# A hybrid two-layer kernel on one core: the down and last projections by token ranges, with a range's norms placed beside the next range's products, and 1026 tokens instead of 1044 in the feed-forward

## The reference

```python
h = h + rms_norm(mix, mix_post_g)
xn = rms_norm(h, ffn_pre_g)
gu = xn @ w_up                                  # 1024 -> 2 * 2816
g = causal_dwconv(gu[..., :D_FF], ffn_conv_w, ffn_conv_b)       # 3 taps
f = (gelu(g, approximate=True) * gu[..., D_FF:]) @ w_down       # 2816 -> 1024
h = h + rms_norm(f, ffn_post_g)
x = h[:, N_META:]                               # first_block returns this
u = _rmsnorm(x, norm_w) @ w_in                  # the second layer
...                                             # gated linear attention, RWKV
x = x + merged @ w_out
return _rmsnorm(x, final_norm_w)
```

## Time and profile before

| | |
|---|---|
| median of 3 runs | 2700.62 us (2700.24 to 2700.97) |
| the profiled execution: its time, its span | 2705.07 us, 2703.3 us |
| mean granted clock of TensorE | 0.961 |
| busy: PE, PEld | 2486.1 us (92%), 1514.5 us (56%) |
| busy: DVE, POOL, ACT | 1265.1, 1102.5, 896.2 us |
| DMA | 164.79 MB, 61 GB/s on average |

### The profile page before, as it was taken

How to read it: one execution, slowest core, us unless ns; L and a number is a source line. 1 busy time by engine, 2 the same in 40 slices (tenths; PEclk the granted TensorE clock), 3 DMA queues, 4 the chain that set the end, 5 groups by cost and what they waited for, 6 DMA issues and landing times. The chain is left out here.

```text
span 2703.3 us, 44126 instructions
## 1 busy us (share of the span) xinstructions
PE 2486.1 (92%) x18196; PEld 1514.5 (56%) x18196; DVE 1265.1 (47%) x1204; ACT 896.2 (33%) x1528; POOL 1102.5 (41%) x784
## 2 busy tenths in 40 slices
PE   6999988999999989989999997999479999979986
PEld 3666655666666545656666664444124444568842
DVE  5665763434344455675444442000567746226513
ACT  3126754555555563441111111000144432114301
POOL 6453236565555642025444443333365433100141
PEclk8999999999999989999999998999789999979998
DMA  2122110000000013321111111110023541123231
GB/s 104 55 68 82 55 48 24 25 24 25 24 17 24 9 46 105 126 84 55 48 53 47 54 47 51 43 53 32 29 85 94 155 133 40 55 82 84 68 123 62
DMA packets 100039, 164.79 MB, mean 61 GB/s; under 512 B 25488, under 2 KB 71712, under 8 KB 98480
## 3 DMA queue, kind: packets, MB, share of 16 engines
q1 hardware_dynamic: 99888, 162.64, 18.9%
HBM read 136.86 MB, written 25.76 MB: 60 GB/s over the span
## 5 line engine op out<-in xcount | busy, mean ns | idle before, releaser
L1398 DVE TENSOR_TENSOR_SCAN att_kept<-att_keep 128x143 f32<-128x143 f32 (+7 forms) x128 | 171.0, 1342 | 315.0 <-ACT att_keep L1315 315.0
L214 PE MATMUL ps<-x_hi,whi_z 128*128 128x348 f16 x1008 | 313.0, 311 | 0.2 <-POOL wlo_z L188 0.2
L216 PE MATMUL ps<-x_hi,wlo_z 128*128 128x348 f16 x1008 | 312.6, 310 | 0.0
L215 PE MATMUL ps<-x_lo,whi_z 128*128 128x348 f16 x1008 | 312.1, 310 | 0.0
L1162 POOL TENSOR_TENSOR att_beta<-att_beta,att_kept 128x256 f32<-128x256 f32 (+7 forms) x128 | 195.6, 1528 | 221.7 <-DVE att_kept L1398 200.8
L2155 PE MATMUL ps<-second_x_hi,whi_second 128*128 128x512 f16 x480 | 183.9, 383 | 14.5 <-POOL second_x_lo L316 13.4
L1195 PE MATMUL ps<-x_hi,whi_z 128*128 128x348 f16 x576 | 181.1, 314 | 14.0 <-POOL wlo_z L1152 9.4
L2156 PE MATMUL ps<-second_x_lo,whi_second 128*128 128x512 f16 x480 | 183.7, 383 | 0.0
L2157 PE MATMUL ps<-second_x_hi,wlo_second 128*128 128x512 f16 x480 | 183.5, 382 | 0.0
L1196 PE MATMUL ps<-x_lo,whi_z 128*128 128x348 f16 x576 | 180.4, 313 | 0.0
L1197 PE MATMUL ps<-x_hi,wlo_z 128*128 128x348 f16 x576 | 180.4, 313 | 0.0
(11 more groups left out here) (483 smaller groups left out, 5829.0 us busy)
## 6 DMA issues: line engine op xcount, KB each, us to landing
wraw_z<-in_w_up SPq DMA_DIRECT2D x44, 512.0 KB, 3.5
wraw_second<-in_w_second SPq DMA_DIRECT2D x30, 512.0 KB, 3.6
wraw_z<-in_w_qkv SPq DMA_DIRECT2D x24, 512.0 KB, 3.6
wraw_down<-in_w_down SPq DMA_DIRECT2D x16, 704.0 KB, 4.0
second_work<-parked_units SPq DMA_DIRECT2D x8, 1280.0 KB, 7.0
seg<-dt_a_sums SPq DMA_DIRECT2D x18, 512.0 KB, 3.9
wraw_z<-in_w_out SPq DMA_DIRECT2D x18, 512.0 KB, 3.7
wraw_out<-in_w_out SPq DMA_DIRECT2D x18, 512.0 KB, 3.6
```

Of the source, the lines that this page charges most:

```text
L214: nc.tensor.matmul(out, hi, xhi, start=(k == 0), stop=False)
L215: nc.tensor.matmul(out, hi, xlo, start=False, stop=False)
L216: return nc.tensor.matmul(out, lo, xhi, start=False, stop=(k == L.parts * L.kb - 1))
L1398: nc.vector.tensor_tensor_scan(out[:, 1:t.keys], x, x, 1.0, ALU.mult, ALU.min).then_inc(s_scan, 1)
```

## The change

The part of the program before `w_out` is as it was. From there on:

1. **1026 tokens.** `w_out` and `w_up` are computed for the last two learned tokens and the 1024 real ones, three thirds of `FT` = 342 columns instead of 348; the products and their numbers are otherwise the same. The cuts of `f` are done in two halves of 512 tokens.
2. **Down by ranges.** `ffn_down_phase` replaces `linear_phase` and both norm phases. A unit is a weight column block and a token range: 8 units for range A (tokens 0 to 511), blocks 7 and 6 for B and C together (512 columns), six units of 256 columns for B, six for C. A unit's weights come in three parts (8, 8 and 6 blocks of 128) that each unit loads anew, except the one where the block stays the same; cuts are ACT's (high) and DVE's (low), in a ring of four; the first parts are loaded, the very first also cut, in `ffn_up_phase`. The steps of both norms of a range, by the `link_` functions, stand in the lists of ACT and DVE between the cuts of the units after it. Range C's are in `second_in_phase`, beside its first two weight blocks (`first_linears`). Both norms' sums over features are added up on ACT and DVE first, so a sum is one product with ones. `parked_h` is written range by range.
3. **The last projection by ranges.** In `rwkv_units_phase` the products of `w_out_2` run over tokens 0 to 511, 512 to 767, 768 to 1023, all eight blocks each; the weights' halves are all kept. The final norm of a range is beside the next range's products, and a range's result leaves block by block. The first two weight blocks are cut within the units (`c == NUNIT - 1`).
4. All semaphores of the second layer's last phase are cleared at the end of the program. The set-up of `x11` in `rwkv_units_phase` comes after two others.

```diff
+F0 = META - 2
+FT = (T - F0) // NT
+FW = NT * FT
...
             @block.sync
             def _(sp):
                 stream_weights(sp, L, 2 * FFB)
+                for s in range(SLOTS):
+                    sp.wait_ge(L.cut, 2 * FFB - SLOTS + s + 1)
+                    sp.dma_start(Ld.raw[:, s, :], Ld.w[0][:, s * SEQ:(s + 1) * SEQ]).then_inc(Ld.landed[s], 16)
             @block.gpsimd
             def _(pool):
                 cut_weights(nc, S, pool, L, 2 * FFB)
+                pool.wait_ge(L.products, done(L, 2 * FFB - SLOTS))
+                cut_first(nc, S, pool, Ld, 1)
...
+F_KEPT = 16
+LAST = SEQ // 4
+RANGES = {"A": slice(0, BANK), "BC": slice(BANK, SEQ), "B": slice(BANK, SEQ - LAST), "C": slice(SEQ - LAST, SEQ)}
+DOWN_UNITS = [(b, "A") for b in range(DB)] + [(DB - 1, "BC"), (DB - 2, "BC")]
+DOWN_UNITS += [(b, "B") for b in range(DB - 2)] + [(b, "C") for b in range(DB - 2)[::-1]]
+DOWN_PARTS = ((0, 8), (8, 16), (16, FFB))
+END_OF_A, END_OF_B = DB - 1, 2 * DB - 1
...
+            @block.sync
+            def _(sp):
+                for i in range(SLOTS):
+                    nc.sync.sem_inc(s_landed[i], 16)
+                for i in range(SLOTS, NL):
+                    if i >= RING:
+                        sp.wait_ge(s_cut, i - RING + 1)
+                    b, q = DOWN_LOADS[i]
+                    k0, k1 = DOWN_PARTS[q]
+                    sp.dma_start(w_raw(i), A["w_down"][b][:, k0 * P:k1 * P]).then_inc(s_landed[i % RING], 16)
+                    if i == fresh(END_OF_B - 1)[0]:
+                        sp.wait_ge(CA.added, DB)
+                        sp.dma_start(parked_h[:, :, RANGES["A"]], down[:, :, RANGES["A"]]).then_inc(s_parked_h, 16)
+                for s in range(SLOTS):
+                    sp.wait_ge(s_cut, NL - RING + s + 1)
+                    sp.dma_start(L.raw[:, s, :], L.w[s]).then_inc(L.landed[s], 16)
+                L.fetched = True
+                sp.wait_ge(CB.added, DB)
+                sp.dma_start(parked_h[:, :, RANGES["B"]], down[:, :, RANGES["B"]]).then_inc(s_parked_h, 16)
+                sp.wait_ge(s_parked_h, 2 * 16)
...
+                for u in range(len(DOWN_UNITS)):
+                    if u >= 6:
+                        pe.wait_ge(s_sq, u - 5)
+                    if u == END_OF_A + 3:
+                        link_sum(nc, S, pe, CA, 1)
+                    part(u, 0)
+                    if u == END_OF_A + 1:
+                        pe.wait_ge(s_acc, sums_by(END_OF_A))
+                        link_sum(nc, S, pe, CA, 0, ssq[:, RANGES["A"]])
+                    if u == END_OF_B + 1:
+                        pe.wait_ge(s_acc, sums_by(END_OF_B))
+                        link_sum(nc, S, pe, CB, 0, ssq[:, RANGES["B"]])
+                    if u == END_OF_B + 4:
+                        link_sum(nc, S, pe, CB, 1)
+                    part(u, 1)
+                    part(u, 2)
...
+                squares = {END_OF_A + 1: (CA, ((0, 1), (2, 3))), END_OF_A + 2: (CA, ((4, 5, 6), (7,), ())),
+                           END_OF_B + 1: (CB, ((), (0,), (1,))), END_OF_B + 2: (CB, ((2,), (3,), (4,))), END_OF_B + 3: (CB, ((5,), (6, 7), ()))}
+                roots = {(END_OF_A + 1, 0): (CA, 0), (END_OF_A + 3, 0): (CA, 1), (END_OF_B + 1, 1): (CB, 0), (END_OF_B + 4, 1): (CB, 1)}
+                highs = {END_OF_A + 3: (CA, ((0,), (1, 2), (3,))), END_OF_A + 4: (CA, ((4,), (5,), (6,))), END_OF_A + 5: (CA, ((7,), (), ())),
+                         END_OF_B + 4: (CB, ((), (), (0, 1))), END_OF_B + 5: (CB, ((2,), (3,), (4,))), END_OF_B + 6: (CB, ((5, 6), (7,)))}
...
+                def low(i):
+                    dve.wait_ge(s_whi, i + 1)
+                    nc.vector.scalar_tensor_tensor(w_lo(i), w_raw(i), WSCALE, w_hi(i), ALU.mult, ALU.subtract).then_inc(s_cut, 1)
...
-        with nc.sbuf_tensor("ffn_out", [P, DB, SEQ], F32) as down:
-            with Phase(nc) as layer:
-                L = linear_buffers(nc, layer, A["w_down"], 0, FFB // 2, "down", parts=2)
-                linear_phase(nc, S, L, lambda k: (S.fhi[:, k, :], S.flo[:, k, :]), DB, down, 2, BANK, META)
-            norm_phase(nc, S, "ffn_post", down, "ffn_post_g", DB, SEQ, ("add", S.h[:, :, META:T]), 2, BANK)
-
+        S.xhi, S.xlo = x
+        Ls = linear_buffers(nc, second, A["w_second"], 0, DB, "second", like=Lz)
+        down = second.enter_context(nc.sbuf_tensor("ffn_out", [P, DB, SEQ], F32))
+        ffn_down_phase(nc, S, A, Lz, Ld, Ls, down, rows, parked_h, s_parked_h)
...
+                    if i == 2 * SLOTS:
+                        sp.wait_ge(C.added, DB)
+                        sp.dma_start(parked_h[:, :, SEQ - LAST:SEQ], W.high[:, :, SEQ - LAST:SEQ]).then_inc(s_parked_h, 16)
...
+                def first_linears():
+                    nc.tensor.sem_inc(L.cut, SLOTS)
+                    pe.wait_ge(L.cut, SLOTS)
+                    link_sum(nc, S, pe, C, 0, ssq[:, SEQ - LAST:SEQ])
+                    for at, end in ((0, BANK), (BANK, SEQ - LAST), (SEQ - LAST, SEQ)):
+                        for i in range(SLOTS):
                             for j in range(DB):
-                                last = product(n, j)
-                    last.then_inc(s_lin, 1)
+                                if i == 0 and end == SEQ:
+                                    pe.wait_ge(C.low, j + 1)
+                                last = product(i, slice(at, end), j)
+                            if end == SEQ:
+                                last.then_inc(s_lin, 1)
+                            if i == 0 and end == SEQ - LAST:
+                                link_sum(nc, S, pe, C, 1)
...
+                first_linears()
                 for i in range(SECOND_B + 2):
-                    if i < SECOND_B:
+                    if i < SLOTS:
+                        pass
+                    elif i < SECOND_B:
...
+                link_root(nc, S, act, C, 0, DB)
+                for n in range(DB):
+                    link_square(nc, act, C, n)
+                link_root(nc, S, act, C, 1, DB)
+                for n in range(DB):
+                    link_high(nc, act, C, n)
...
+        spans = ((0, BANK), (BANK, BANK + BANK // 2), (BANK + BANK // 2, SEQ))
+        width = lambda i: spans[i][1] - spans[i][0]
+        done_units = (4, 6, 8)
...
+                    if c == NUNIT - 1:
+                        sp.wait_ge(s_glo, GLA_HEADS)
+                        fetch_first(sp, L)
+                        sp.dma_start(back, parked_h).then_inc(s_back, 16)
...
+                for i in range(len(spans)):
+                    for b in range(DB):
+                        sp.wait_ge(s_fin, i * DB + b + 1)
+                        sp.dma_start(out[:, b, toks(i)], back[:, b, toks(i)]).then_inc(s_result, 16)
+                sp.wait_ge(s_result, 16 * DB * len(spans))
...
+                    if c == NUNIT - 1:
+                        cut_first(nc, S, pool, L)
                     if c == NUNIT:
-                        cut_first(nc, S, pool, L)
+                        pool.wait_ge(s_yd, NUNIT)
+                        pool.wait_ge(s_rrc, NUNIT)
+                        cut(SLOTS)
...
+                def output(i, b):
+                    u = i * DB + b
+                    ps = bank(u % 4)[:, 0:width(i)]
+                    pe.wait_ge(L.cut, b + 1)
+                    if u >= 4:
+                        pe.wait_ge(s_res, u - 3)
+                    for j in range(DB):
+                        if b == 0 and j == RWKV_P:
+                            pe.wait_ge(s_lo, done_units[i])
+                        hi, lo = (w(b)[:, j * P:(j + 1) * P] for w in (w_hi, w_lo))
+                        xhi, xlo = (x[:, j, toks(i)] for x in merged)
+                        nc.tensor.matmul(ps, hi, xhi, start=(j == 0), stop=False)
+                        nc.tensor.matmul(ps, hi, xlo, start=False, stop=False)
+                        last = nc.tensor.matmul(ps, lo, xhi, start=False, stop=(j == DB - 1))
+                    last.then_inc(s_po, 1)
...
+                for i in range(len(spans)):
+                    for b in range(DB):
+                        output(i, b)
+                        if i == 0 and b == 0:
+                            variances(NUNIT - 1)
+                        if i and b == 1:
+                            square_sums(i - 1)
+                square_sums(len(spans) - 1)
...
+                for i in range(len(spans)):
+                    for b in range(DB):
+                        residual(i, b)
+                        if b >= 2:
+                            more(i, b - 1)
+                        if i and b >= 3:
+                            final(i - 1, b - 3)
...
-            rwkv_units_phase(nc, S, D, W, plast, L, merged, parked_h, back)
-        res = S.h_flat[:, 0:DB * SEQ].rearrange("p (a n) -> p a n", a=DB)
-        norm_phase(nc, S, "final", back, "final_norm_w_2", DB, SEQ, ("to", res, out, s_result), 2, BANK)
```

(21 more changed lines are left out.)

471 lines of the change are left out of this document (321 added, 150 removed).

## The result

2614.09 us (median of 4 runs, 2611.27 to 2615.34), against 2700.43 us for the kernel before in the same comparison (median of 4, 2695.04 to 2700.97): a ratio of 0.9671, 95% interval 0.9657 to 0.9685. That is 86 us less; forecast were 107, a time of 2594 in a range of 2576 to 2618. The direction and the range held. The time lies outside the forecast's own band (2584 to 2604), in the one that had been given to rival B (2604 to 2622). The profiled execution has a span of 2613.2 us, 90.1 less than before.

The account below looks back on a forecast made before the run. The prediction took PE, busy 92% of the span, as the bound. Its terms for fewer columns, shorter handovers and added costs summed to -107.0 us, from 2700.6 to 2593.6, say 2594 us; range 2576 to 2618.

Parts of the forecast that it names:

- rival B: Later handovers: norm steps on DVE beside POOL take twice the time, units pay POOL's cuts; 2604 to 2622 us; chance 0.17.
- Step 1: w_out and w_up: 6 columns fewer in each of 4320 products; -10.8 us, down to -9 possible.
- Step 2: Up to down: weights cut early, PE waits only for the tail of f, 4.5 us standing; -10.4 us.
- Step 3: Down itself: narrower products, products with ones and block meetings, +4.1 us; weight stream, DVE's cuts and norms taken as hidden.
- Step 4: Last down product to low_ranks(0): 31.4 us plus 2.4 slow start instead of 100.5; -66.7 us.
- Step 5: Second input phase to the units: POOL's clears remain, x11 set-up moves behind two others; taken 0.
- Steps 6 and 7: Units: POOL's two weight block cuts, +1 us; units to w_out_2: standing and slow start go, -10.1 us.
- Steps 8 and 9: Last products: more products, sums and cuts, +2.8 us; end after the last product 16.0 instead of 32.86 us, -16.9 us.
- C: Weight stream falls behind in down: a 256-column unit takes 10.8, not 7.2 us; +43, 2637 us; chance 0.04.
- D: Narrow 256-column products don't hide their weight load; +123 us, 2717 us, slower than before; chance 0.01.

Follow-up runs that it names:

- e7: The changed kernel with thirds of 346 columns instead of 342 in w_out and w_up; 2615.03 us (one run).
- e2: The changed kernel with POOL cutting the first two w_up blocks only after DVE's last low cut of w_out; 2610.86 us (one run).
- e1: The changed kernel with the norms' squares and high cuts behind the next weight part's high cut in ACT's list in down; 2597.27 us, ratio to before 0.9610.
- e3: The changed kernel with the four low-rank products between the halves of the third weight block, not ahead of it; 2607.98 us (one run).
- e8: The changed kernel with POOL's first two w_out_2 cuts moved back behind the eighth unit's place in its list; 2621.64 us (one run).
- e4: The changed kernel with 51 of the last phase's 83 semaphores cleared while the last products still run; 2607.03 us (one run).
- e5: The changed kernel with the edits of e1, e3 and e4, and only w_up's first block cut in the out phase, after DVE's last cut; 2585.34 us, ratio 0.9565.

## Why the prediction was right, and where it was off

- **Step 1, columns:** right for the up phase (-7.4 of -7.9, and e7's slope). In the out phase the prediction allowed for "waits of its own" and a loss of 2 us, and it was 4.5 in the first profile. 2.1 us of it are PE's wait at the phase's end, which grew from 2.4 to 4.5. The term left out was POOL beside DVE (2.07 and 3.13 us for cuts of 1.22). Before, one of the two was stretched as well (1.23 and 2.05 us); after, both. e2 shows that it is POOL; that they meet the other way round because the products are shorter fits all eight traces in which POOL is not held back, with 342, 346 and 348 columns. The other 2.5 us are the half-clock stretches that four of six traces of this list don't have (e2), so this much was chance, in the execution and not in the change.
- **Step 2, up to down:** right, 4.58 us of standing against 4.5.
- **Step 3, down:** the step that failed: "The norms are wanted only at the next stage. Cost 0, with up to 3 in the range." The amounts of work were right (DVE 115 us of 245), and the pitch and the count of products too. I compared DVE's work with PE's time and did not follow the order of the two lists: each square on ACT and each weight cut are links of one loop, of 3.4 us where 2.4 are to be had. And one of the norms' products stands in PE's own list, so a late norm is not only late at the next stage: it stopped PE for 4.4 us. Cost: 11.2 us over the term, where the range had allowed 3; e1 takes 11.9 away, and then down is 233.6 where the forecast sum has 234.3.
- **Step 4, to `low_ranks(0)`:** the chain as worked, tanh's wait included (5.2 of 5.3), but 4.9 us of standing at its head and not 1.7, since the last evacuation was queued behind late norm steps, and 5.1 us of products at clock 0.50 behind that. This too was step 3's error: with the loop open, 31.5 us against a forecast of 31.4. e3 shows that the tanh wait could be filled, and that the chain behind it has room. (As written, the terms of this step give 23.8 and not 23.5 for block 0, and 24.7 and 6.45 add up to 31.2, not 31.4; neither slip matters here.)
- **Step 5:** 1.0 us sooner, the bound that the row had given; not separately tested.
- **Steps 6 and 7:** e8 has both: the handover's 7.80, the slow start's 2.35, of which only 1.2 is seen in the stage, and nothing for the cuts in the units, where I had taken 1. The units were 2.4 us shorter than before even so. In their first 29 us the mean granted clock was 0.86 and before 0.76; that fits a shorter slow start. e8 has 0.86 too, so it is not the place of the cuts; what made it shorter was not tried.
- **Steps 8 and 9:** right within 1 us; PE's wait for a cut in step 8 was 1.5 where I had taken about 1. The price of a clear, read from 64 of them in a row, came out at 71 ns (e4).
- **The rivals:** B gave the right time for a reason that is only partly its own. POOL beside DVE did cost something, in the out phase, where it had not been placed, and not in the chains it named. C is ruled out by e1. D is ruled out by the pitch: 256-column products follow one another at 109 ns, with a weight load of some 97 ns for each. The Trainium skill's rule ("TensorE: Matmul & The Clock Gate", "What overlaps and what doesn't") would make that, by an estimate from these two times, over 200 ns; this trace contradicts it as well. (The prediction's 242 ns for 348 columns by that rule should be 244.5, from 147.5 and 97.)

So the range was hit by a sum whose largest errors were not foreseen. The mechanisms that carry the gain (no block of norms between the projections, weights cut ahead of both handovers, a short end) came out as worked: those four rows of the table (up to down, the handover, the units, the end) gave 101 us of the 103 forecast. Against that stood 17 us in down and its handover from one loop that the prediction had put at nothing, and the time stayed in the range by 4 us because other terms were 5 us better and the top of the range had been set for another reason, rival B. With that loop opened (e1) the time is 2597, inside the forecast's own band.

## What to carry to other kernels

- Where two engines feed a third in alternation, add up the round trip along their in-order lists, not each engine's work: an item that waits for the other engine must not stand ahead of the item that the other engine waits for. The order of one list was worth 17 us here (e1).
- A small step of a side chain that sits in the bounding engine's list (here a product with ones) makes that whole chain critical; place it late enough that its input is certainly there.
- Put POOL's wide operations where DVE is idle or has slack. Beside each other DVE's operations took 1.7 times (2.07 for 1.22 us) to over 4 times (2.44 for 0.56) as long, and moving the clash moved part of the cost (e2, e5).

## What had not been expected of the hardware

- DVE's low cut of 1024 columns took 1.22 us alone and 2.05, 2.07 or 3.13 beside POOL's cuts, and POOL's scaling of a block 1.04 when it came first and 2.12 when DVE did. A lead of 0.01 to 0.04 us decided which of the two was stretched, and with it 2 us of PE's wait. The order repeated in every trace of the same program, but from the kernel before it could not be predicted, nor could the stage to 2 us.
- After the same stand of PE in the out phase the mean granted clock over 7.57 us was 0.55 in one execution of the same program and 0.82 in another, with 26 products done and 41. It is most of the 2.5 us that are the largest difference between stages of the same program here.
- Holes inside down repeat from one execution to the next to 0.01 us: the one of 4.42 or 4.43 us and the one of 2.02 or 2.03 are in all seven traces of changed kernels without e1's edit, though these differ elsewhere.
